# Five groups of seven products in the first three down stages, with half of each group's weight sums made by adding transfers

## The reference

```
# block 1, hidden width 8192 (four chunks of 2048 in the kernel)
h = h + jnp.square(jax.nn.relu(hn @ ffn_w1[i])) @ ffn_w2[i]
gate = jax.nn.sigmoid(rms_norm(h, norm_ple[i]) @ ple_w_gate[i])
h = h + (p[i] @ ple_w_proj[i]) * gate
...
# block 2, hidden width 5632 (chunks of 2048, 2048 and 1536 in the kernel)
return (jax.nn.silu(gate) * val) @ w_down
```

## Time and profile before

| what | value |
|---|---|
| median of three runs | 2196.92 us (2195.22 to 2197.0) |
| profiled execution, its own time | 2197.45 us |
| its span | 2195.6 us |
| TensorE busy | 2180.6 us, 99% |
| VectorE busy | 1566.8 us, 71% |
| ScalarE busy | 1133.7 us, 52% |
| POOL busy | 710.6 us, 32% |
| moved by transfers | 414.35 MB, mean 189 GB/s |

### The profile page before, as it was taken

How to read it: one execution, slowest core, us unless ns; L and a number is a source line. 1 busy time by engine, 2 the same in 40 slices (tenths; PEclk the granted TensorE clock), 3 DMA queues, 4 the chain that set the end, 5 groups by cost and what they waited for, 6 DMA issues and landing times.

```text
span 2195.6 us, 34076 instructions
## 1 busy us (share of the span) xinstructions
PE 2180.6 (99%) x11511; PEld 1863.4 (85%) x11511; DVE 1566.8 (71%) x2187; ACT 1133.7 (52%) x1720; POOL 710.6 (32%) x625
## 2 busy tenths in 40 slices
PE   9999999999999999999999999999999999999998
PEld 8888988888888888888887887788888888888887
DVE  6877766558658757755868667568778777787775
ACT  6445555555445445444555455465555455554553
POOL 3202320361362263153000033005554355533531
PEclk9999999999999999999999999999999999999999
DMA  7665335556556556565555654545555655555554
GB/s 253 233 224 172 109 135 187 167 188 211 191 182 210 187 187 205 206 195 194 181 192 178 229 168 141 192 163 181 189 195 184 201 198 193 187 191 197 200 207 148
DMA packets 118084, 414.35 MB, mean 189 GB/s; under 512 B 12896, under 2 KB 18048, under 8 KB 117472
## 3 DMA queue, kind: packets, MB, share of 16 engines
q1 hardware_dynamic: 111600, 401.37, 54.4%
q10 hardware_dynamic: 6384, 11.70, 1.7%
HBM read 409.29 MB, written 2.15 MB: 187 GB/s over the span
## 4 chain that ended last, share of the span: by engine, by line
PE 91%; DVE 4%; POOL 2%; issue 2%; ACT 1%; DMA 0%; POOLq 0%; DVEq 0%; ACTq 0%
PE bank L607 31%; PE bank L615 16%; PE bank L941 6%; PE bank L943 6%; PE bank L942 6%; PE bank L664 3%; PE bank L666 3%; PE bank L665 3%; DVE wboth L1307 1%; POOL bias L2661 1%; PE bank L720 1%; PE bank L1269 1%; PE bank L1267 1%; PE bank L1268 1%; PE bank L721 1%
## 5 line engine op out<-in xcount | busy, mean ns | idle before, releaser
L1307 DVE TENSOR_TENSOR wboth<-raw,wboth 128x1024 fp32r<-128x1024 f32 (+1 forms) x756 | 954.2, 1267 | 470.5 <-ACT wboth L2157 462.2
L2157 ACT CAST wboth<-raw 128x1024 fp32r<-128x1024 f32 (+1 forms) x756 | 773.0, 1034 | 468.4 <-PE bank L943 123.9
L607 PE MATMUL bank<-A,wboth 128*128 128x512 f32 x2928 | 705.4, 392 | 0.5 <-DVE wboth L1307 0.3
L607 PEld LDWEIGHTS bank<-A,wboth 128*128 128x128 f32 x2928 | 536.8, 188 | 105.3 <-issue 1.3
L615 PEld LDWEIGHTS bank<-A,wboth 128*128 128x128 f32 x2928 | 376.7, 191 | 14.8
L615 PE MATMUL bank<-A,wboth 128*128 128x256 f32 x2928 | 384.0, 283 | 0.0
L941 PE MATMUL bank<-wboth,H 128*128 128x512 f32 x508 | 197.9, 389 | 1.2 <-DVE wboth L1307 1.2
L942 PE MATMUL bank<-wboth,H 128*128 128x512 f32 x508 | 197.7, 389 | 0.0
L943 PE MATMUL bank<-wboth,H 128*128 128x512 f32 x508 | 197.6, 389 | 0.0
L2661 POOL TENSOR_TENSOR PT<-z,rs 128x256 f32<-128x256 f32 x88 | 92.5, 1052 | 263.4 <-DVE z L1338 261.4
L2661 POOL TENSOR_TENSOR bias<-z,rs 128x256 f32<-128x256 f32 x64 | 104.7, 1635 | 197.8 <-DVE z L1338 109.4
(11 more groups left out here) (387 smaller groups left out, 3161.2 us busy)
## 6 DMA issues: line engine op xcount, KB each, us to landing
raw<-wstream SPq DMA_DIRECT2D x756, 512.0 KB, 3.3
bias<-bias_rows ACTq DMA_DIRECT2D x6, 512.0 KB, 5.4
x<-xrows ACTq DMA_DIRECT2D x1, 2048.0 KB, 10.6
bias<-grows ACTq DMA_DIRECT2D x2, 1024.0 KB, 6.5
out<-x SPq DMA_DIRECT2D x8, 256.0 KB, 2.1
x<-xT SPq DMA_DIRECT2D x7, 256.0 KB, 5.2
pA<-bias_rows ACTq DMA_DIRECT2D x2, 512.0 KB, 6.9
Sm<-grows ACTq DMA_DIRECT2D x1, 1024.0 KB, 6.9
```

The lines of the kernel that those rows point to most:

```text
L607: last = nc.tensor.matmul(bank(j)[:, :], whi[:, s, cols(i)], moving(j, k), start=(k == 0), stop=(k == K - 1))
L1307: V.tensor_tensor(wlo[:, s, 0:w], raw[:, s, 0:w], whi[:, s, 0:w].bitcast(F32), ALU.subtract).then_inc(lo_ready, 1)
L2157: C.copy(whi[:, s, 0:w], raw[:, s, 0:w]).then_inc(hi_ready, 1)
```

## The change

- FIRST gets SECOND's layout: groups at pieces 8, 12, 20, 24 and 28, three mixed pairs (2, 4, 6), and the banks taken in at the places of SECOND.
- `t_first` is gone from DVE and from POOL, in the FIRST and in the SECOND stages. In its place POOL issues two transfers for each group. `t_load` copies both column halves of piece x from HBM over sums 0 and 1 (512 KB). When it has landed, `t_add` adds the second column halves of pieces x and x+1 to them, from HBM (`accum_op=ALU.add`, 512 KB). `t_second` and `t_highs` wait for the landing of `t_add` (`t_sum`).
- `t_load` of a group waits for the first of the two lows of the group before. In a FIRST stage that of group 0 is issued ahead of the `mix_low`s, and its `t_add` behind them; in a SECOND stage, where sums and mixed rows share a buffer, both come behind the `mix_low`s.
- `corners` of a FIRST stage wait for the main banks or the sides as in SECOND, and the first one comes after the `t_add` of group 2. Waits for `corners` in `mains_in` are gone.
- The mix of the pair 6 is made after the last row of its group of four hidden rows, and so after the last hidden row of the chunk.
- `proj` uses the other set of banks first, since the sides of the last FIRST stage are now taken in later.
- `dn_half` shares the semaphore that `t_sum` had.

```diff
@@ -188,7 +188,7 @@
-FIRST = Pairing(((3, 5), (3, 5)), sides=12, mains=17, last_sides=28)
+FIRST = Pairing(((4, 6), (2, 4, 6)), sides=14, mains=16, last_sides=32)
 SECOND = Pairing(((4, 6), (2, 4, 6)), sides=14, mains=16, last_sides=32)
@@ -398,7 +398,8 @@
         mix_sum, mix_hi, mix_ready = Again(acc_step, BLK), Again(pc_hi, 2 * KVG), Again(pad_zero, 1)
-        t_sum, t_more, t_hi = Again(c_taken, 5 * KVG), Again(cpad_zero, 1), Again(c_exp, KVG)
+        t_more, t_hi = Again(cpad_zero, 1), Again(c_exp, KVG)
+        t_loaded, t_sum = sem("t_loaded"), sem("t_sum")
         t_lo, t_used = Again(c_shift, KVG), Again(c_scores, KVG)
@@ -1047,10 +1048,11 @@
             for f in range(4):
-                pe.wait_ge(*banks_taken.at(8 * (FF_CHUNKS - 1)))
-                if f == 2:
-                    pe.wait_ge(z_ready, 4 + UB["proj"])
-                rows_group(PB["proj"] + f, PB["proj"] + f, UB["proj"] + 2 * f, UB["proj"] + 2 * f, 2, pA, free=True, upper=(f < 2))
+                if f < 2:
+                    pe.wait_ge(z_ready, 4 + UB["proj"] - 2 + 2 * f)
+                else:
+                    pe.wait_ge(*banks_taken.at(8 * (FF_CHUNKS - 1)))
+                rows_group(PB["proj"] + f, PB["proj"] + f, UB["proj"] + 2 * f, UB["proj"] + 2 * f, 2, pA, free=True, upper=(f > 1))
             chunk(FF_CHUNKS - 1)
@@ -1755,33 +1757,21 @@
                 at = pairing(c)
-                summed = [0] if is_down2(c) else range(len(at.groups))
-                steps_of.update({at.at_x[g] - 4: lambda g=g: t_first(c, g) for g in summed})
                 steps_of.update({x - 3: lambda x=x, g=g: t_second(c, x, g) for x, g in at.x_at.items()})
                 ahead = {x + 2: lambda g=g: t_lows(c, g) for x, g in at.x_at.items()}
-                ahead.update({x: lambda g=g: dve.wait_ge(*t_sum.at(2 * group_of(c, g) + 2)) for x, g in at.x_at.items() if g not in summed})
                 steps_of.update({at.sides: lambda: sides_in(c, 0), at.mains: lambda: mains_in(c, 0, range(4)), at.last_sides: lambda: sides_in(c, 1),
...
-            def t_first(c, g):
+            def t_second(c, i, g):
                 _, fd, o = stage_at(c)
-                i = pairing(c).at_x[g]
-                x, y = PB[fd] + i, PB[fd] + i + 1
+                q = PB[fd] + i + 1
+                y = raw[:, q % SLOTS, :]
                 if g or not is_chunk(c, 0):
                     dve.wait_ge(*t_lo.at(2 * group_of(c, g)))
-                if is_down2(c):
-                    dve.wait_ge(*mix_ready.at(mix_count(c, len(SECOND.mixed))))
-                dve.wait_ge(raw_landed[x % SLOTS], o * 256 + (x // SLOTS + 1) * 16)
-                V.tensor_tensor(sums_at(c)[:, 0, :], raw[:, x % SLOTS, 0:WIDE], raw[:, x % SLOTS, WIDE:], ALU.add).then_inc(t_sum.sem, 1)
-                dve.wait_ge(raw_landed[y % SLOTS], o * 256 + (y // SLOTS + 1) * 16)
-                V.tensor_tensor(sums_at(c)[:, 1, :], raw[:, x % SLOTS, WIDE:], raw[:, y % SLOTS, WIDE:], ALU.add).then_inc(t_sum.sem, 1)
-
-            def t_second(c, i, g):
-
-                y = raw[:, (PB[stage_at(c)[1]] + i + 1) % SLOTS, :]
-                dve.wait_ge(*t_sum.at(2 * group_of(c, g) + (2 if is_down2(c) else 1)))
+                dve.wait_ge(raw_landed[q % SLOTS], o * 256 + (q // SLOTS + 1) * 16)
+                dve.wait_ge(t_sum, 16 * group_of(c, g) + 16)
                 V.tensor_tensor(sums_at(c)[:, 2, :], sums_at(c)[:, 0, :], y[:, WIDE:], ALU.add).then_inc(t_more.sem, 1)
@@ -1800,8 +1790,8 @@
                     dve.wait_ge(*corners_added.at(c * 6 + 3 * cp))
-                if cp and is_down2(c):
-                    dve.wait_ge(z_ready, 4 + UB[fd] + 8)
+                if cp:
+                    dve.wait_ge(z_ready, o * 24 + (4 + UB[fd] + 8))
                 one, five, six, seven = (side_bank(c, cp, j)[:, :] for j in range(4))
@@ -1824,12 +1814,8 @@
                     dve.wait_ge(z_ready, o * 24 + (4 + UB[fd] + 4))
-                    if not is_down2(c):
-                        dve.wait_ge(*corners_added.at(c * 6 + 3))
                 elif js[0] == 0:
                     dve.wait_ge(*first_half.at(c + 1))
-                    if not is_down2(c):
-                        dve.wait_ge(*banks_taken.at(c * 8 + 8))
                 else:
@@ -1869,7 +1855,7 @@
                     dve.wait_ge(z_ready, 4 + UB["proj"] + 2 * f)
-                V.tensor_copy(yN[:, 0, f * WIDE:f * WIDE + WIDE], psum[(UB["proj"] + 2 * f) % 4 + (4 if f < 2 else 0)][:, :]).then_inc(z_ready, 1)
+                V.tensor_copy(yN[:, 0, f * WIDE:f * WIDE + WIDE], psum[(UB["proj"] + 2 * f) % 4 + (4 if f > 1 else 0)][:, :]).then_inc(z_ready, 1)
             rows_body(PB["proj"], PB["proj"], 1, 4, proj_in)
@@ -2412,7 +2398,7 @@
-                act.wait_ge(*t_sum.at(2 * group_of(c, g) + 2))
+                act.wait_ge(t_sum, 16 * group_of(c, g) + 16)
                 if g or not is_chunk(c, 0):
@@ -2441,7 +2427,7 @@
                 act.wait_ge(z_ready, 4 + UB["proj"] + 2 * f + 1)
-                C.copy(yN[:, 1, f * WIDE:f * WIDE + WIDE], psum[(UB["proj"] + 2 * f + 1) % 4 + (4 if f < 2 else 0)][:, :]).then_inc(z_ready, 1)
+                C.copy(yN[:, 1, f * WIDE:f * WIDE + WIDE], psum[(UB["proj"] + 2 * f + 1) % 4 + (4 if f > 1 else 0)][:, :]).then_inc(z_ready, 1)
             act.wait_ge(*t_used.at(group_of(FF_CHUNKS - 1, 0)))
@@ -2710,32 +2696,45 @@
                                         ALU.subtract).then_inc(ff_ready, 1)
-                        if j % 2 and 2 * it + j // 2 in FIRST.mixed and not is_last(c):
-                            mix(c, FIRST.mixed.index(2 * it + j // 2), tB, j - 1, j)
+                    for j in range(2) if not is_last(c) else ():
+                        if 2 * it + j in FIRST.mixed:
+                            mix(c, FIRST.mixed.index(2 * it + j), tB, 2 * j, 2 * j + 1)
                 if not is_last(c):
...
-                for n in range(len(pairing(c).mixed)):
+                at = pairing(c)
+                if not is_down2(c):
+                    t_load(c, 0)
+                for n in range(len(at.mixed)):
                     mix_low(c, n)
-                for g in range(1, len(SECOND.groups)) if is_down2(c) else ():
-                    if g == SECOND.used(0) + 1:
+                if is_down2(c):
+                    t_load(c, 0)
+                t_add(c, 0)
+                for g in range(1, len(at.groups)):
+                    t_load(c, g)
+                    t_add(c, g)
+                    if g == at.used(0):
                         corners(c, 0)
-                    t_first(c, g)
-                for cp in (1,) if is_down2(c) else range(2):
-                    corners(c, cp)
-
-            def t_first(c, g):
+                corners(c, 1)
+
+            def t_load(c, g):
                 _, fd, o = stage_at(c)
-                i = SECOND.at_x[g]
-                x, y = PB[fd] + i, PB[fd] + i + 1
-                pool.wait_ge(*t_lo.at(2 * group_of(c, g)))
-                pool.wait_ge(raw_landed[x % SLOTS], o * 256 + (x // SLOTS + 1) * 16)
-                G.tensor_tensor(sums_at(c)[:, 0, :], raw[:, x % SLOTS, 0:WIDE], raw[:, x % SLOTS, WIDE:], ALU.add).then_inc(t_sum.sem, 1)
-                pool.wait_ge(raw_landed[y % SLOTS], o * 256 + (y // SLOTS + 1) * 16)
-                G.tensor_tensor(sums_at(c)[:, 1, :], raw[:, x % SLOTS, WIDE:], raw[:, y % SLOTS, WIDE:], ALU.add).then_inc(t_sum.sem, 1)
+                i = o * 64 + (PB[fd] + pairing(c).at_x[g])
+                if g or not is_chunk(c, 0):
+                    pool.wait_ge(*t_lo.at(2 * group_of(c, g) - 1))
+                if is_down2(c) and g == 0:
+                    pool.wait_ge(*mix_ready.at(mix_count(c, len(SECOND.mixed))))
+                pool.dma_start(sums_at(c)[:, 0:2, :], wstream[ds(i, 1)].rearrange("a p (f n) -> p (a f) n", f=2)).then_inc(t_loaded, 16)
+
+            def t_add(c, g):
+
+                _, fd, o = stage_at(c)
+                i = o * 64 + (PB[fd] + pairing(c).at_x[g])
+                pool.wait_ge(t_loaded, 16 * group_of(c, g) + 16)
+                pool.dma_start(sums_at(c)[:, 0:2, :], wstream[ds(i, 2), :, WIDE:].rearrange("a p n -> p a n"), accum_op=ALU.add).then_inc(t_sum, 16)
@@ -2757,11 +2756,7 @@
-                if is_down2(c):
-                    pool.wait_ge(*banks_taken.at(c * 8 + (4 + 4 * cp)))
-                else:
-                    _, fd, o = chunk_at(c)
-                    pool.wait_ge(z_ready, o * 24 + (4 + UB[fd] + (8 if cp else 4)))
+                pool.wait_ge(*banks_taken.at(c * 8 + (4 + 4 * cp)))
                 for t, f, src, op in ((1, 0, corner, ALU.subtract), (0, 1, cross, ALU.add), (1, 1, cross, ALU.add)):
```

More of the change, by code:

```diff
@@ L419, in program @@
         fin_rs, fin_out, out_done = (sem(n) for n in ("fin_rs", "fin_out", "out_done"))
-        dn_half = sem("dn_half")
+        dn_half = Again(c_taken, 5 * KVG)
         def main_bank(c, cp, j):
@@ L1283, in down2 @@
                             last = rows_of(k, 0)
-                        last.then_inc(dn_half, 1)
```

(3 more changed lines are left out.)

## The result

The changed kernel takes 2363.4 us (median of 4 runs, 2362.5 to 2364.0) against 2196.7 (4 runs, 2195.2 to 2197.0): ratio 1.076, 95% interval 1.0745 to 1.0771. That is 166.6 us slower, where +22.8 was forecast, and outside the range.

What follows compares the result with a forecast made beforehand. TensorE, busy 99% of the span, was taken as the bound. Waits of 26.35 us, less 2.04 and 1.56, gave +22.75 on the profiled 2197.45, 0.5 less against the median: 2219.7 us; range 2194 to 2250, likeliest case 2201 to 2247.

Steps and rivals of the forecast that it cites:

- nine matmuls fewer: One more group in each of three FIRST stages removes 3 x 3 matmuls of 0.2267 us, a gain of 2.04 us.
- The spare time of group 3: In SECOND's group 3, TensorE was to stand still for C - 6.8 us.
- C: Time from a group's first low to the landing of the next group's t_add; taken as 8.0 us, bounds 6.2 and 11.8.
- The price of C: Step pricing the two chained transfers from SP's 512 KB weight loads: 4.0 us each, the add's second read not priced.
- Group 0 in FIRST: Waits at group 0: A - 1.35 in the first FIRST stage, A - 3.6 in the second; 3.35 us over three stages.
- A: Time for the landing of t_add at group 0 of a FIRST stage, taken as 4.0 us.
- Edits at nothing: Side edits (proj banks, corners semaphore, dn_half, sides at piece 32) priced at zero; proj at most 0.5 us, left out.
- Removed: adds on DVE and POOL: FIRST's DVE loses 6.6 us of adds against 3.8 for the fifth group; hidden by TensorE, not in the sum.
- the 1.56 us of the first FIRST stage: The first FIRST stage's excess over the next two, expected to vanish: taken as -1.56 us, other bound 0.
- The starved stream: Weight loads held back so that group 2 or the splits wait for them; left out of the forecast, no size.
- the adding transfer is slow: Rival: C from 9.5 us up, giving 2247 us at 9.5 and 2290 at 11.8; chance 0.2.
- The quick one: Rival: transfers as quick as lone loads, C up to 7.0 us, giving 2195 to 2201.5 us; chance 0.27.

Runs made afterwards that it cites:

- e5: The e1 kernel with sums 0 and 1 of group 2 alone made by t_load and t_add in each of the five stages; 2200.5 us.
- e6: The e1 kernel with sums 0 and 1 of group 3 alone made by t_load and t_add in each of the five stages; 2246.2 us.
- e3: The changed kernel with t_add copying over sums 0 and 1 in place of adding to them; 2318.5 us.
- e10: The changed kernel with t_load left out in groups 1 to 4, t_add issued in its place; group 0 keeps both; 2258.9 us.
- e1: The changed kernel's layout without its transfers: sums 0 and 1 made by DVE in group 0, by POOL in the others; 2201.4 us.
- e9: The e1 kernel with the three mixes of a FIRST stage back directly behind their second hidden row; 2200.6 us.
- e4: The changed kernel with sums 0 and 1 of even groups in a second buffer, so each transfer pair is issued a group earlier; 2229.2 us.
- e8: The e4 kernel with FIRST's group 0 load before the last four hidden rows, its add before the mix_lows, and the mixes back in place; 2211.0 us.
- e7: The changed kernel's transfers in the SECOND stages only, FIRST stages by engines as in e1; 2260.5 us.
- e2: The changed kernel without t_add, so sums 0 and 1 lack their second half; 2204.3 us.

## Why the prediction was wrong

**Right.** The nine matmuls fewer. The mechanism: two chained transfers stop DVE at `t_second`, DVE's split stops TensorE, once in groups 0, 1, 3 and 4 and never in group 2 (e5, e6). The spare time of group 3, too: C - 6.8 gives 6.35 us for C = 13.15, and TensorE waited 6.6 above; over the five stages it gives 33.1 and 32.5 were measured. And that the kernel gets slower.

**The step that failed is "The price of C".** 4.0 us for each of two transfers, 8.0 in sum, measured 4.6 and 8.0, and with the wake-ups 13.1 to 14.5 in the links. My upper bound, 11.8, was two crowded loads of SP, and C lies above it, since the adding was "not priced" though it "pulls towards the high end". The 5.3 us between 8.0 and 13.3 are: 0.6 for `t_load`; 4.0 for `t_add`, of which about 2 are the adding (2.1 alone, 1.6 in the medians, e3) and about 2 the moment at which it is issued (5.9 against 8.0, e10; that the bursts of weight loads make this difference is argued, not shown); and 0.7 of wake-ups, which the sum had at nothing. The bound should have had an adding transfer at a copy's time and as much again for the second read.

**A loss that was in no rival: the clock.** The forecast took a wait for its own length. With C = 13.3 its formulas give 20.0 us a FIRST stage (groups 1, 3, 4) and 26.6 a SECOND one (with group 0), and with the 8.3 us measured at group 0 of FIRST and shortly before it (6.8 and 1.5), 138 us in all: 2197 - 3.6 + 138 = 2331. Some 32 us are missing, and nearly all of them are the slow clock. Busy time in the stages rose by 49.6 us although the nine matmuls, 2.0 us, are gone: the twenty slow stretches cost some 52 us, 2.6 each and not the 3.4 of half of 6.83, as all but one begin while TensorE still waits, by 1.0 to 3.1 us. Some 22 of the 52 come back: behind the slow stretches of groups 0 and 3 the next group waits for its transfers anyway, and the waits of groups 1 and 4 are 4.5 us in the mean where the formula has 6.75. That leaves 30; about 2 more lie in the two stretches between FIRST stages. e6 has the clock by itself, 17.0 us over five waits.

**Group 0 in FIRST** was sized at A - 1.35 and A - 3.6 with A = 4.0. It waits 6.6 to 7.1 us. Both terms failed: A was 9.2 to 9.8, and `t_load`, "hidden" behind three `mix_low` of 2.05, took 5.9 to 6.2 us while the three took 3.8, so that `t_add` went out 19.6 us into the second FIRST stage and not 16.3.

**Edits at nothing, and terms of gain.** Under "Removed: adds on DVE and POOL" the fifth group was given its two adds and two subtractions, but not the third mix and third `mix_low` that pieces 2, 4, 6 bring where 3 and 5 were; with the issue of `t_load` ahead of them, three `mix_low` in a row delay DVE's split, and TensorE waits 1.5 us in each FIRST stage. So neither the 2.04 us of the matmuls nor the 1.56 us of the first FIRST stage shows as a gain in e1, e5 or e9: five groups with sums made by engines are 4 to 5 us slower than the kernel before. The banks of `proj` and the other edits behind the last FIRST stage did cost nothing: from its end to the first SECOND stage it is 727.0 us before and 727.2 after. The starved stream, which was left out, was rightly left out as far as the runs show: in the SECOND stages of e4 the transfers run at a share of 0.84 with TensorE never idle.

**The rivals.** That the adding transfer is slow was the right one, at 0.2 and with a price cut off at 2290. The quick one is refuted by C itself.

## What to carry to other kernels

A transfer in a serial link is to be priced with all that stands in the link: its own kind (adding or copying), when it is issued against the bursts of the stream beside it, and the step after it. In the SECOND stages the same 20 transfers cost nothing when issued a group ahead into a second buffer (83.8 and 84.0 us a stage), and 64 us when each had to wait for the group before (115.2 and 116.6): look for the distance before the duration. And a long wait of TensorE is to be priced at more than its length: in e6 a wait of 5.6 us cost 3.4 more by the slow stretch that came with it.

## What the runs showed of the hardware

- An adding transfer of 512 KB from memory, issued by POOL, with no load beside it: 5.7 and 5.8 us from issue to landing; a copy of the same bytes and rows: 3.7. POOL is busy 1.2 us issuing the add, 0.7 for that copy and 0.6 for `t_load`.
- The clock: in the five stages it fell to 0.50 for 3.41, 6.83 or 10.24 us with each wait of 3.3 us and more in the traces of all runs. With waits of 2.0 to 3.2 us it did so at some places and not at others (in e8 with one of 2.5, not with three of 2.3 to 2.4; in e3 with one of 2.0, not with two of 3.2). With a single wait of 1.6 us or less it never did; in e7 it did with one of 1.0 and one of 1.5 us a microsecond apart.
- DVE and POOL hold each other up when their element-wise operations run side by side: a split of 1.22 us took 3.8 beside three `mix_low` back to back, ending 1.1 us behind the last of them (e2), 1.34 beside the end of one (e4), and 1.96 and 2.31 beside three in e1, where the third `mix_low` took 2.28 in place of 1.3.
- The weight stream and POOL's transfers ran together at a share of 0.84 and 268 GB/s over a whole stage with TensorE never idle (e4).
